# Attention scores with bias and negative maximum in one VectorE instruction a head, and four state products summed on TensorE, in the first layer of a two-layer block

## The reference

```python
# attention, block of 128 queries against 256 keys (the block before and its own)
scores = jnp.where(valid, q @ k.T * scale + bias, NEG_INF)
m = jnp.maximum(jnp.max(scores, axis=-1, keepdims=True), sink)
p = jnp.exp(scores - m)
p = p / (jnp.sum(p, axis=-1, keepdims=True) + jnp.exp(sink - m))
out = p @ v

# S5: h is the complex state of a diagonal recurrence over the tokens
y = (jnp.einsum('blgp,gcp->blgc', h_re, c_re)
     - jnp.einsum('blgp,gcp->blgc', h_im, c_im) + d_skip * uf)

# PEER: each token picks 8 x 16 = 128 experts out of 16384
a = jnp.einsum('cd,ced->ce', xb, u_tab[eb])
w = gate * gelu(a)
out = jnp.einsum('ce,ced->cd', w, v_tab[eb])
```

## Time and profile before

| | us |
|---|---|
| median of 3 runs | 3291.14 |
| lowest, highest | 3282.91, 3292.65 |
| the profiled execution, its own time | 3288.82 |
| its span, first to last instruction | 3287.2 |
| PE busy | 2450.0 (75%) |
| DVE busy | 2320.3 (71%) |
| ACT busy | 1330.0 (40%) |
| POOL busy | 1125.5 (34%) |
| mean DMA rate over the span | 394 GB/s |

### The profile page before, as it was taken

One profiled execution on the slowest core, in us unless ns is written; L12 is line 12 of the kernel. 1 busy time (PEld: TensorE's weight loads), 2 busy tenths in 40 slices (PEclk: granted clock), 3 DMA queues, 4 the chain that ended last, 5 costly groups with the idle time before them and its releaser, 6 DMA issues.

```text
span 3287.2 us, 40578 instructions
## 1 busy us (share of the span) xinstructions
PE 2450.0 (75%) x14052; PEld 1035.0 (31%) x14052; DVE 2320.3 (71%) x5500; ACT 1330.0 (40%) x3602; POOL 1125.5 (34%) x1038
## 2 busy tenths in 40 slices
PE   8969679786797777878787869878887655555554
PEld 3433233223332233335442426423333211111111
DVE  8439783878838787475875695887866777777644
ACT  2114442444424443243583343367744433333322
POOL 0012342324323243232343343343433444443432
PEclk9979889887898988989888879878888877777777
DMA  8899999999999999999999999999999999999997
GB/s 247 309 366 408 410 382 404 414 402 404 387 405 418 410 401 386 407 390 385 377 376 396 390 408 396 392 414 412 371 418 406 418 419 420 415 416 410 419 420 329
DMA packets 214057, 1295.01 MB, mean 394 GB/s; under 512 B 26934, under 2 KB 30294, under 8 KB 82776
## 3 DMA queue, kind: packets, MB, share of 16 engines
q0 software_dynamic: 148320, 1076.50, 81.1%
q1 hardware_dynamic: 64860, 213.81, 17.1%
q10 hardware_dynamic: 672, 2.12, 0.2%
HBM read 1289.62 MB, written 2.71 MB: 393 GB/s over the span
## 4 chain that ended last, share of the span: by engine, by line
PE 34%; DMA 26%; DVE 22%; issue 9%; ACT 4%; POOL 3%; POOLq 0%; ACTq 0%; another core or an unknown queue 0%; DVEq 0%
DMA ring<-in_k_uv,idx 11%; PE ps L1722 11%; DMA ring<-in_k_vu,idx 10%; DVE ring L415 9%; PE ps L1802 9%; PE ps L2096 6%; DMA wsl<-in_k_wu 3%; POOL ring L2400 3%; PE ps L2106 2%; DVE big L470 2%; ACT L1249 2%; DMA wsl<-in_k_wmod 1%; PE ps L1779 1%; PE ps L1977 1%; DVE pers L470 1%
## 5 line engine op out<-in xcount | busy, mean ns | idle before, releaser
L1722 PE MATMUL ps<-ring,diag 64*64 64x512 f32 x8192 | 1254.0, 737 | 481.0 <-ACT diag L1249 458.1
L415 DVE CUSTOM_DVE_ANT_0 ring<-ring,xn 128x1024 f32<-128x1024 f32 x1024 | 1238.7, 1221 | 454.0 <-DMA ring<-in_k_vu,idx 234.2
L2400 POOL DMA_INDIRECT ring<-in_k_vu,idx x514 | 562.3, 1094 | 1131.2 <-DVE aw L415 656.6
L2400 POOL DMA_INDIRECT ring<-in_k_uv,idx x510 | 557.1, 1092 | 957.7 <-DVE aw L415 690.4
L1722 PEld LDWEIGHTS ps<-ring,diag 64*64 64x64 f32 x8192 | 309.1, 157 | 1239.7 <-ACT diag L1249 719.0
L1249 ACT ACTIVATE aw<-aw 128x2 f32<-128x2 f32 x512 | 103.6, 202 | 1049.6 <-DVE aw L415 1048.2
L1802 PE MATMUL ps<-wsl,xT 128*128 128x512 f32 x896 | 430.7, 626 | 23.2 <-DMA wsl<-in_k_wu 19.4
L1249 ACT ACT_TABLE_LOAD x339 | 434.9, 1283 | 22.4 <-issue 10.4
L1249 ACT ACTIVATE diag<-gid,aw 128x64 f32<-128x64 f32 x1024 | 311.7, 342 | 311.2 <-PE ps L1722 294.3
L1249 ACT ACTIVATE gid<-ident,gate 128x64 f32<-128x64 f32 x1024 | 292.4, 332 | 0.0
L1802 PEld LDWEIGHTS ps<-wsl,xT 128*128 128x128 f32 x896 | 168.1, 197 | 283.1 <-issue 240.0
(11 more groups left out here) (264 smaller groups left out, 2132.8 us busy)
## 6 DMA issues: line engine op xcount, KB each, us to landing
wsl<-in_k_wu SPq DMA_DIRECT2D x342, 512.0 KB
wsl<-in_k_wmod SPq DMA_DIRECT2D x40, 512.0 KB
ring<-in_k_vu,idx POOLq DMA_INDIRECT x514
ring<-in_k_uv,idx POOLq DMA_INDIRECT x510
ring<-in_k_wmod SPq DMA_DIRECT2D x8, 512.0 KB, 11.1
wsl<-in_k_wu SPq DMA_DIRECT2D x8, 280.0 KB
hres<-in_x SPq DMA_DIRECT2D x4, 512.0 KB, 6.1
pers<-L1d POOLq DMA_DIRECT2D x8, 256.0 KB, 14.5
```

The costliest lines, as they stand in the source:

```text
L415: V(v.tensor_tensor_reduce(u_row(s), u_row(s), xn[:, n % 3, :], 1.0, 0.0, ALU.mult, ALU.add, aw[:, b, k:k + 1]), ("dot", s))
L1722: r = t.matmul(PA[half][64 * q:64 * q + 64, :], diag[64 * half:64 * half + 64, s % (2 * PAIR), :], v_row(s)[64 * half:64 * half + 64, 512 ...
L2400: Q(p.indirect_dma_start(out=both_rows(s), out_offset=None, in_=tab, in_offset=bass.IndirectOffsetOnAxis(ap=idx[:, n % 2, k:k + 1], axis=0 ...
```

## The change

Three things, all within the mids of tiles 1 to 3.

Scores: instead of two additions, one reduction and two small operations for four heads, VectorE runs one `tensor_tensor_reduce` a head. It writes -(score + bias) and, in the same instruction, the minimum over the 256 keys and the negated sink, which is the negative maximum that the exponential takes as its bias. The exponential scales by -1. The negated sinks (`nsnk`) are formed once in tile 0.

State: `s5_out` forms the four products (re cos, -im sin, re sin, im cos) and no longer adds them in pairs. TensorE takes all four as operands, 16 products instead of 8 in `s5y`. Only the last column of the state is added on VectorE, in two operations of 128x4.

Order on TensorE: the scores of group g + 1 are issued right behind the products with V of group g, and no longer at the start of group g + 1.

```diff
@@ first_tile, once
+                V(ts(nsnk, snk, -1.0, None, ALU.mult, None))
@@ att_scores
-                hs = slice(4 * g, 4 * g + 4)
                 V.stage("att")
                 V.wait_ge("a_sc", n, g)
                 V.wait_ge("bias", 0)
-                for b in range(2):
-                    V(tt(sc1[:, 2 * b:2 * b + 2, 0:256], PS[b].rearrange("p (a b) -> p a b", a=2)[:, :, 0:256],
-                         bias1[:, 4 * g + 2 * b:4 * g + 2 * b + 2, 0:256], ALU.add))
-                step()
-                V.wait_own()
-                V(v.tensor_reduce(mx1[:, hs], sc1[:, :, 0:256], AXX, ALU.max))
-                chained(lambda: tt(mx1[:, hs], mx1[:, hs], snk[:, hs], ALU.max))
-                chained(lambda: ts(nm1[:, hs], mx1[:, hs], -1.0, None, ALU.mult, None), ("a_nm", n, g))
+                for r in range(4):
+                    h = 4 * g + r
+                    if r == 2:
+                        step()
+                    V(v.tensor_tensor_reduce(sc1[:, r, :], PS[r // 2][:, 256 * (r % 2):256 * (r % 2) + 256],
+                                             bias1[:, h, :], -1.0, nsnk[:, h:h + 1], ALU.add, ALU.min,
+                                             nm1[:, h:h + 1]), *([("a_nm", n, g)] if r == 3 else []))
@@ s5_out
                 V.wait_own()
+                if n:
+                    V(tt(b0, b2, ec, ALU.mult))
+                    V(v.scalar_tensor_tensor(b1, b3, -1.0, es, ALU.mult, ALU.mult))
+                    step()
+                    V(tt(b2, b2, es, ALU.mult))
+                    step()
+                    V(tt(b3, b3, ec, ALU.mult), ("s_h", n, c))
+                    V.wait_own()
+                    hre, him = [hst[:, z, 4 * c:4 * c + 4].unsqueeze(2) for z in range(2)]
+                    V(tt(hre, b0[:, :, 127:128], b1[:, :, 127:128], ALU.add))
+                    V(tt(him, b2[:, :, 127:128], b3[:, :, 127:128], ALU.add))
+                    step()
+                    return
                 V(tt(b0, b2, ec, ALU.mult))
                 V(tt(b1, b3, es, ALU.mult))
@@ mid1 on VectorE, the end
-                V(tt(mx1, snk, mx1, ALU.subtract), ("a_sk", n))
+                V(tt(mx1, snk, nm1, ALU.add), ("a_sk", n))
@@ mid1 on ScalarE
-                        S(act(sc1[:, r, :], sc1[:, r, :], ACT.Exp, bias=nm1[:, h:h + 1],
+                        S(act(sc1[:, r, :], sc1[:, r, :], ACT.Exp, scale=-1.0, bias=nm1[:, h:h + 1],
@@ s5y
-                b0, b1, _ = state_bufs(n)
+                b0, b1, b2 = state_bufs(n)
+                parts = ((0, b0), (0, b1), (1, b2), (1, b3)) if n else ((0, b0), (1, b1))
                 for j in range(4):
-                    for z, bb in ((0, b0), (1, b1)):
+                    for i, (z, bb) in enumerate(parts):
@@ mid1 on TensorE
-                    scores1(n, g)
-                    if g:
+                    if g == 0:
+                        scores1(n, 0)
+                    else:
                         s5y(n, g - 1)
...
                     T(x, ("a_pv", n, g))
+                    if g < 3:
+                        scores1(n, g + 1)
```

More of the change, by code:

```diff
@@ L194, in build @@
         snk, o = carve(pers, o, 16)
+        nsnk, o = carve(pers, o, 16)
         assert o <= PERS, o
@@ L1945, in s5y @@
                 for j in range(4):
-                    for z, bb in ((0, b0), (1, b1)):
+                    for i, (z, bb) in enumerate(parts):
                         x = t.matmul(PS[2][32 * j:32 * j + 32, 0:128], CT[:, 16 * z + 4 * c + j, :], bb[:, j, :],
-                                     start=(z == 0), stop=(z == 1), tile_position=(0, 32 * j))
+                                     start=(i == 0), stop=(i == len(parts) - 1), tile_position=(0, 32 * j))
                 T(x, ("s_y", n, c))
```

## The result

The changed kernel takes 3294.18 us in the median of 20 runs, the kernel before 3286.70 us in 20 runs on the same chip: a ratio of 1.0023, 95% interval 1.0013 to 1.0033. That is 7.5 us more, within the 0.3% that a measurement of this kernel tells from no change by the prediction's own bound, and on the slower side. The forecast was 20 us less.

A forecast was written before the change was run, and what follows sets the result against it. VectorE's lateness was taken to hold the gathers back in the mids; nine passages of 2.4 us give 21.6, less 1.5, so 20 us off: 3271 us against the 3291.1 median, range 3262 to 3287.

The forecast's parts named there:

- What bounds the kernel: In the three mids, VectorE's queue and its waits set the pace, holding transfers at 382 to 387 GB/s.
- the room: Most the three mids could gain at undisturbed transfer rates: 22.5 us against 416 GB/s, 25.2 against 420.
- (a): Scores on VectorE: four new instructions take 1.5 us a group instead of 2.73, saving 1.2, bounds 0.7 and 1.4.
- (b): State on VectorE: 2.95 us a group instead of 4.24, saving 1.3, or 0.8 if one operation ran at half rate.
- (c): State's products on TensorE: doubled from 0.59 to 1.2 us, adding 0.6 to 0.7 us a group, twelve groups.
- The sum, as a new walk round the loop: Mid loop from one L757 to the next: 28.0 us instead of 30.4, 2.4 saved in each of nine passages.
- (d): Scores moved ahead of three vmm slots on TensorE: those vmm end 1.92 us later, nine times in the kernel.
- R3: Rival, chance 0.08: slower, VectorE stays late through costly instructions or state-product waits, late vmm delay gathers; 10 us, 17 at most.
- R1: Rival, chance 0.20: VectorE faster, but GpSimd waits for the later vmm; gain 9 us, bounds 2 and 12, 3282 us.

The follow-up runs named there:

- e7: Changed kernel with the V products three steps later in TensorE's order, behind more vmm: 3271.00 us, ratio 0.9937 to the kernel before.
- e11: Kernel before with one score instruction a head on VectorE and the V products three steps later: 3261.27 us, ratio 0.9924 to the kernel before.
- e12: Changed kernel with V products three steps later and state products taking turns over the column groups: 3261.47 us, ratio 0.9922 to the kernel before.
- e2: Kernel before with only the new scores part, one instruction a head on VectorE: 3275.57 us, ratio 0.9957 to the kernel before.
- e5: Changed kernel with the sixteen state products taking turns over the column groups: 3289.11 us, ratio 1.0003 to the kernel before.
- e3: Kernel before with only the state edit, no sums on VectorE and 16 products on TensorE: 3289.03 us, ratio 0.9998 to the kernel before.
- e9: Changed kernel with six unread matmuls in TensorE's idle time ahead of the V products: 3272.80 us, ratio 0.9959 to the kernel before.
- e4: Changed kernel with the scores put back to the start of each group, both VectorE edits kept: 3277.34 us, ratio 0.9969 to the kernel before.
- e1: Kernel before with only the scores moved behind the V products of the previous group: 3286.43 us, ratio 0.9988 to the kernel before.
- e13: Changed kernel without its state edit, keeping one instruction a head and the moved scores: 3288.87 us, ratio 1.0002 to the kernel before.
- e14: Kernel before with six unread matmuls in TensorE's idle time ahead of the V products: 3267.99 us, ratio 0.9952 to the kernel before.

## Why the prediction was wrong

**What bounds the kernel** was read rightly: the rate in the mids was the room, VectorE and what it waits for was the pace, and once the loop is short the mids do reach 406 to 417 GB/s (e7), with 25 us in all (e11, e12) against a room of 22.5 to 25.2. The changed kernel itself did what the prediction's last sentence names as its failure: the rate in the mids did not rise, and VectorE idled.

**(a), scores on VectorE**, was right. The new instruction is 0.40 us from start to start (422.20 to 422.61 to 423.01 in the changed kernel's timeline), 1.6 us for four where 1.5 was taken. Alone it gives 14 us (e2), and its predicted share was 9 x 1.2 = 11.

**(b), state on VectorE**, was right too: from 415.83 to 419.67 less a dot is 2.7 us, where 2.95 was taken (its terms add up to 3.0), and L736 takes 684 ns, which is full rate. The Trainium skill's halved throughput for that operation (Vector Engine (DVE) Microarchitecture Reference, the section on points that are easy to get wrong) is not what this instruction does here.

**(c), state's products on TensorE**, failed in size: 2.39 us from start to start, not 1.2. "Twice that" took the rate of two products a column group for four in a row. e5 shows that it is the order: in turn they take 1.01. Its price is 5 to 7 us in the changed kernel (e5); that the whole state edit gives nothing by itself (e3) fits with this eating the saving of (b), but no run has the state edit alone with its products in turn.

**The sum, as a new walk round the loop**, is the step that failed, in the term "TensorE: V products to 416.71, scores 1.92 to 418.63, three slots 3.72 to 422.35". The scores' 1.92 was measured behind the vmm, where the clock was 1.00, and then used in front of them, where it is 0.50. They take 3.7 there, the three slots take 5.0 for 3.7. With (c) the walk comes out 11.1 us from the scores' start to the slots behind the state's products (418.38 to 429.49), where the prediction had 6.9 (416.71 to 423.6). From the copy to the state's inputs it is 18.9 us (413.99 to 432.87) instead of 15.1 (412.31 to 427.4); the rest of the loop is 12.88 us, exactly as forecast. So the loop of 31.8 us instead of 28.0 is off by this chain alone, and where the scores did run at full clock, in the third loops of e9, the loops are 27.4 to 28.3. The row to ask was not in its rows: the granted clock over those 4 us, and the V products' own 3.65 us out of 6.67 us of idle time, which is in the earlier trace rows. The Trainium skill (TensorE: Matmul & The Clock Gate, the section on HAM oscillation) warns of this very shape, work that restarts after a wait at the lower clock; the traces here agree (0.50 after 7.29 us idle, 1.00 in group 2 of e9 with the wait filled), and the prediction did not weigh it.

**(d) and the rivals.** The prediction saw the mechanism and gave it little weight: it put the first late vmm at 4.4 + 1.9 + 1.2 = 7.5 us behind L757, with 10 us of gathers still to be moved. In the changed kernel the vmm only start 8.1 us behind the copy (413.99 to 422.09), and the gather behind the first of them is issued at 10.9 (424.88); before it was issued at 7.2 (412.31 to 419.50). The 3.7 us between are what the scores take there at the low clock; at full clock they would be 1.9. The gathers in flight do not last that long: the hole of 234 GB/s.

What happened is nearest to R3, slower, to which the prediction gave 0.08: 7.5 us where it had put 10. Its first condition, new instructions of over 0.7 us, did not hold. Its second did, a wait for the state's products so long that VectorE stays as late as before: 3.4 us in the loop above and 26.4 over the three mids. Its signs hold too: GpSimd's waits for vmm grew from 43.8 to 65.6 us over the three mids while those for dots shrank from 169.4 to 161.7 (in tile 1 alone it is the other way round, where the view puts the 7.5 us down to a dot), and 373, 381 and 381 GB/s lie under 382. What the move costs, 18 us by e4 against the changed kernel, is near R3's bound of 17. Only R3's picture, that the delay comes through the gathers, is half of it: VectorE waits longer for TensorE's products than for gathers. R1 (0.20) has the same late releases with VectorE faster; its gain of 2 to 12 us did not come.

Together: 14 us from (a), about 0 from the state edit, and a move that gives about 4 us alone but takes 15 to 18 once VectorE is fast. The three do not add up (-14 + 0 - 4 would be -18, measured +7.5). The traces show why the move has less to give: TensorE's wait for L751, the idle time of 3.10 in the earlier trace rows, is 27.3 us over the three mids before, 16.4 in e2, 0.2 in e4 and 0 in e1. The VectorE edits and the move remove the same wait. The changed kernel against e4, and e13 against e2, show that the loss needs the move. That the low clock lengthens the chain is shown by e9, within one run. How much of the 15 to 18 us is the clock and how much the order stays open: filling the wait gives the changed kernel 0.64% (e9) and the kernel before, without the move, nearly as much, 0.48% (e14), and no run has e4 with the wait filled.

## What to carry to other kernels

A duration belongs to its place in the queue: before moving work on TensorE, read the granted clock where it goes, and what the engine did ahead of it. When two edits remove the same wait, price each with the other in place, and look at what the second then does to the releases behind it. An engine that waits in order for a late partner should do the work that is ready first; here three steps in the order of one wait were worth more than all three edits together.

## What the runs showed of the hardware

- Added matmuls whose product nobody reads made both kernels faster, by 0.48% (e14) and by 0.64% (e9). TensorE's granted clock in the mids rose from 0.79 to 0.83 (before) to 0.88 to 0.93 (e14), and from 0.76 to 0.78 (changed) to 0.90 to 0.94 (e9); the same sixteen V product records take 3.65 us at 0.50 and 1.97 us at 1.00.
- Sixteen products of 128x32 weights and 128 columns in float32, 32 records, take 2.39 us when four in a row add into one column group and 1.01 us when the groups take turns, both at a clock of 1.00.
- A tensor_tensor_reduce of 256 columns with one source in PSUM takes 480 ns, and the next starts 0.40 us behind it, with the read of its result between.
